# Two-block transformer on one core: the filler products of TensorE are taken out

## The reference, cut to what matters

```python
def reference(x, mem, ...):
    x = first_block(x, mem, ...)
    return second_block(x, c_2, positions_2, ...)

# first_block, one layer
h = _rmsnorm(x, norm_mix); proj = h @ w_in
ya, yb, yc = _mla(...), _fox(...), _chunk_rel(...)      # three kinds of attention
x = x + concat(_rmsnorm(ya), _rmsnorm(yb), _rmsnorm(yc)) @ w_o
x = x + _cross(_rmsnorm(x), _rmsnorm(mem), w_cq, w_ckv, w_co)
h = _rmsnorm(x); gate, up = split(h @ w_gu)
x = x + (silu(gate) * up) @ w_down
# second_block, layers 0 and 1
h = rmsnorm(x) * (1 + sc1) + sh1
y = (gating and pooling) if l == 0 else diff_attention(h, ...)
x = x + g1 * y
h = rmsnorm(x) * (1 + sc2) + sh2
x = x + g2 * peer(h, ...)                # 16384 experts, 8 heads, top 16
return rmsnorm(x)
```

## Time and profile before

| | us |
|---|---|
| median of 3 runs | 2436.04 |
| lowest and highest of them | 2429.02, 2436.44 |
| the profiled execution's own time | 2429.68 |
| its span, first to last instruction | 2427.9 |

### The profile page before, as it was taken

One profiled execution on the slowest core, in us unless ns is written; L12 is line 12 of the kernel. 1 busy time (PEld: TensorE's weight loads), 2 busy tenths in 40 slices (PEclk: granted clock), 3 DMA queues, 4 the chain that ended last, 5 costly groups with the idle time before them and its releaser, 6 DMA issues.

```text
span 2427.9 us, 35824 instructions
## 1 busy us (share of the span) xinstructions
PE 2345.9 (97%) x12736; PEld 1975.7 (81%) x12736; DVE 1799.5 (74%) x3774; ACT 1013.8 (42%) x1568; POOL 297.8 (12%) x228
## 2 busy tenths in 40 slices
PE   8998999999999999999999998999999999999998
PEld 7766998669897888888888777698977888888886
DVE  5446787759998777777777766399987777777776
ACT  4433342232343444444444446222334444444443
POOL 0000000026680000000000000266800000000000
PEclk9999999999999999999999999999999999999999
DMA  7414788863215565655656551232155555655653
GB/s 265 158 70 165 288 324 329 342 252 122 87 45 173 175 190 190 191 190 190 190 191 190 204 191 36 104 115 96 44 166 170 190 190 191 190 190 191 190 191 122
DMA packets 97731, 430.07 MB, mean 177 GB/s; under 512 B 11232, under 2 KB 11872, under 8 KB 90720
## 3 DMA queue, kind: packets, MB, share of 16 engines
q1 hardware_dynamic: 97632, 428.75, 51.7%
HBM read 427.66 MB, written 1.05 MB: 177 GB/s over the span
## 4 chain that ended last, share of the span: by engine, by line
PE 83%; DVE 13%; ACT 2%; DMA 1%; issue 1%; SPq 0%; DVEq 0%; ACTq 0%; PEldq 0%
PE ps L507 43%; PE ps L819 15%; PE ps L822 8%; PE ps L552 5%; PE ps L775 4%; DVE HN L1816 4%; DVE HN L1814 3%; PE ps L565 2%; PE ps L602 1%; PE ps L623 1%; DVE arena L1826 1%; DVE ring_rounded L1834 1%; PE ps L737 1%; DMA ring<-in_stream 1%; PE ps L801 1%
## 5 line engine op out<-in xcount | busy, mean ns | idle before, releaser
L507 PE MATMUL ps<-ring_rounded 128*128 128x512 f32 x3072 | 744.0, 392 | 8.6 <-DVE ring_rounded L1834 8.2
L1834 DVE TENSOR_TENSOR ring_rounded<-ring,ring_rounded 128x1024 fp32r<-128x1024 f32 (+1 forms) x688 | 648.6, 959 | 131.1 <-ACT ring_rounded L1234 104.6
L507 PEld LDWEIGHTS ps<-ring_rounded 128*128 128x128 f32 x3072 | 561.4, 189 | 128.1 <-issue 15.0
L819 PE MATMUL ps<-HNHT_rounded,ring_rounded 128*128 128x512 f32 x1632 | 403.3, 389 | 0.0
L819 PEld LDWEIGHTS ps<-HNHT_rounded,ring_rounded 128*128 128x128 f32 x1632 | 306.2, 188 | 63.4
L1240 ACT ACTIVATE ring_rounded<-ring 128x1024 fp32r<-128x1024 f32 x202 | 214.4, 1061 | 231.4 <-PE ps L507 231.4
L507 PE MATMUL ps<-parts 128*128 128x256 f32 (+2 forms) x1184 | 249.2, 301 | 2.3 <-DVE parts L1400 1.5
L822 PEld LDWEIGHTS ps<-HNHT_rounded,ring_rounded 128*128 128x128 f32 x1632 | 222.6, 190 | 15.9
L822 PE MATMUL ps<-HNHT_rounded,ring_rounded 128*128 128x256 f32 x1632 | 227.6, 282 | 0.0
L1231 ACT ACTIVATE ring<-ps 128x256 f32<-128x256 f32 x204 | 78.3, 384 | 341.6 <-PE ps L822 341.6
L1924 DVE TENSOR_TENSOR ring<-ps,ring 128x256 f32<-128x256 f32 x204 | 86.6, 424 | 168.7 <-ACT ring L1231 168.7
(11 more groups left out here) (258 smaller groups left out, 2836.7 us busy)
## 6 DMA issues: line engine op xcount, KB each, us to landing
ring<-in_experts_u SPq DMA_DIRECT2D x256, 512.0 KB, 3.5
ring<-in_experts_v SPq DMA_DIRECT2D x256, 512.0 KB, 3.4
ring<-in_stream SPq DMA_DIRECT2D x45, 2048.0 KB, 8.9
arena<-in_ada SPq DMA_DIRECT2D x96, 512.0 KB, 7.1
arena<-in_keys SPq DMA_DIRECT2D x2, 1024.0 KB, 13.8
ring<-in_stream SPq DMA_DIRECT2D x1, 1792.0 KB, 7.6
ring<-in_stream SPq DMA_DIRECT2D x1, 1664.0 KB, 8.5
ring<-in_stream SPq DMA_DIRECT2D x1, 1040.0 KB, 19.5
```

Of the source, the lines that this page charges most:

```text
L507: mm = pe.matmul(out_, p, q, start=(first and i == 0), stop=(last and i == 2))
L819: pe.matmul(r3(t, 2), exp_uh[:, j % 2, c], ht_both[:, :, k, :], start=(k == 0), stop=False)
L1834: return dve.tensor_tensor(dst, src, h.bitcast(F32), ALU.subtract)
```

## The change

The table of fillers is emptied. `fill` and its calls stay, and issue nothing. No wait, no buffer and no order of other instructions is altered.

```diff
-FILLERS = {("y", 0): 11, ("cross", 1): 8, ("ffn", 1): 8, ("mix_0", 0): 18, ("peer_0", 1): 10, ("sub", 0): 18, ("peer_1", 1): 10,
-           "mix_1": 20, ("gu", 0): 6, ("probs", 0): 6, ("probs", 6): 6, ("probs", 8): 9, ("values", 15): 5}
+FILLERS = {}
```

## The result

Without the fillers the kernel takes 2441.95 us in the median of 8 runs (2437.57 to 2444.99), against 2431.88 us in the median of 8 runs before (2428.58 to 2436.44). The ratio is 1.0040, with a 95% interval of 1.0028 to 1.0051: slower by 10 us, or 0.4%. The profiled execution took 2440.0 us over a span of 2438.2 us, 10.3 us longer than the one before.

A forecast was written before the change was run, and what follows sets the result against it. TensorE, with 83% of the chain that ended last, was taken to bound the kernel. 15 steps at 1.0 us less 1.1 gave +13.9 us, taken as +12 against the median of 2436.04: 2448 us, range 2440 to 2457 us.

The forecast's parts named there:

- The products themselves: Filler products on TensorE: 130 at twelve places worth 0 us, 5 ahead of unit 15's values a gain of 1.1 us.
- all nine places above 3 us: Filler places whose empty stretch exceeds the longest idle time without a fall; five without a fall now get one each.
- the three doubtful ones: ("probs", 0), ("probs", 6) and ("gu", 0), 6 products each, empty for some 2.6 to 3.0 us; two were counted as falls.
- 15 added steps: Steps of some 3.3 us at clock 0.50 added behind filler places, 15 together.
- 7 + 4 + 4: Added steps: 7 new falls, a second step for 4 of them, one step more at each of four existing falls.
- 1.0 us a step: Price of one added step of low clock on TensorE, taken between 0.8 and 1.5 us, nearer the lower end.
- the lower end I had set: Lowest price of a step, 0.8 us: 8 transposes at "y" take 1.91 us in place of 1.09.
- a sign of being wrong: Second and third waits behind a filler place shrink by what the slow transposes took.
- The sum and the median: Whole kernel: 15 - 1.1 = +13.9 us on the profiled 2429.68 us; +12 against the median 2436.04, 2448 us.
- fewer or cheaper falls: Rival, 15%: no falls at doubtful places, few of two steps; 8 steps at 0.8 less 1.1: +5, 2441 us.
- Fillers don't hold the clock: Rival, 6%: idle time after the last filler decides the clock; only unit 15's 1.1 us goes: 2435 us.
- Transposes leave the clock low: Rival, 5%: transposes don't count as activity; eight steps more at the norms' turns, 1.0 us each: 2456 us.

The follow-up runs named there:

- the longer fillers: Kernel before with more fillers at each place and at some further waits, none ahead of the values of unit 15: 2421.07 us, ratio 0.9956.
- the doubled transposes: Kernel before with 270 filler transposes in place of its 135 filler products, at the same places: ratio 0.9996.
- The halves: Two runs against the kernel before: fillers kept only at the six places ahead of "mix_0", ratio 1.0011; kept only from "mix_0" on, ratio 1.0020.
- the runs with transposes: Kernel before with its 135 filler products replaced by transposes of the constant: 135 transposes, ratio 1.0024; 270 transposes, ratio 0.9996.

## Why the prediction was right, and where it was off

*The products themselves cost nothing at twelve places, 1.1 us at the thirteenth.* Right. Blocks are ready when they were ("cross": 178.12 and 178.11 us), and the run without the unit-15 fillers shows the 1.1 us gone and not taken back.

*Falls at all nine places above 3 us, and at two of the three doubtful ones.* Right in number, if the joined stretch counts as two: "cross", "peer_0", ("probs", 8) and "sub" have new ones, and so do ("probs", 6) and, joined in one stretch of 10.2 us, "ffn" and ("gu", 0); ("probs", 0) has none. What I had not counted is that falls elsewhere come and go: two of before (632.0 and 1502.5 us) are missing, one at 1475.1 is new. Nor is a fall tied to its place: the one at "sub" came with the fillers in place, too, in three profiles.

*15 added steps.* The time at 0.50 grew by 93 - 39 = 54 us, 16 steps of 3.4 us. The forecast was 75 to 85 us in the low stretches; they are 85. The make-up differs from the forecast's 7 + 4 + 4: by the stretches, 12 steps lie in new falls at filler places and 5 more in the four that existed, one is added at the spread, and two are missing. That chance took two away and added one helped the total to come out.

*1.0 us a step.* This is the term that was mis-sized. The loss of 10.3 us and the 1.1 us gained beside it make 11.4 us, over 16 steps 0.7 us each; that is just under the lower end I had set, 0.8. Without the three falls that came and went away from the missing fillers (two gains of 1.7 and 1.5 us, a loss of 1.7), 17 steps at filler places cost 12.9 us, 0.76 us each. The lower end was itself the doubling of 8 transposes, and the table of places shows that where a wait for the second block, or for the copies to HT, follows, even that is hidden. The prediction had named this as a sign of being wrong, that later waits shrink by what the slow transposes took; in part it came, as the wait of 0.79 us at "cross" is gone and the one for the second block at "mix_0" is 0.37 us where it was 1.31. One added step at "y" costs nothing, one at "mix_1" 0.34 us. Steps that run into dense products cost more ("peer_0": 2.6 us for two). The other way, the step price is higher: the longer fillers took away about 20 us at 0.50 and 8.6 us of span. Of this 1.1 us is unit 15, and some 1.6 us more would have gone but for the fillers that are too many at the gates, so it is 7.5 / 20 x 3.4 = 1.3 us a step as measured and 1.5 us without that cost; the one fall at the gates was 1.7 us. These falls were the ones in dense work, 93% busy. A price taken from the rows that exist would have been right for removing falls, and was too high for adding them.

*The sum and the median.* With 0.7 in place of 1.0, 16 x 0.7 - 1.1 = +10 us; that it closes shows nothing, as the 0.7 was worked out from this difference. The 2448 us named are 6 us too high, of which 4 us come from the base: the median of the first three runs was 2436.04 us, of eight 2431.88. The profiled execution was nearer the middle than I took it to be. The change itself, +10 us where +12 was named, came nearer than the time; but a step count close by partly opposite chances and a price too high by a third make some of that luck. The measured 2441.95 us is also 2 us above the lower end, and next to the 2441 us of the rival with fewer or cheaper falls.

*Fillers don't hold the clock* fell with the longer fillers. *Fewer or cheaper falls* was wrong in "fewer" and right in "cheaper" (0.7 us a step, its own price being 0.8); its +5 us is refuted, and its time was hit only because the base was 4 us lower. *Transposes leave the clock low* fell with the doubled transposes (ratio 0.9996, where the lack of all fillers gives 1.0040). The Trainium skill ("TensorE: Matmul & The Clock Gate", Part 4) has transposes not counted as activity; here the measurement decides against it.

What stays open: what a single place is worth in time, "sub" above all. The halves add up only within their intervals of about 0.1%, and which of the borderline waits has a fall differs between profiled executions.

## What to carry to other kernels

Work that fills a wait is free while it ends before the wait does, and what it buys is the clock of the work behind the wait; look at the granted clock in a narrow stretch behind each long wait, since a mean of 0.99 hides it. A filler that stops too early can buy almost nothing (0.34 us at "mix_1", where 4.6 us of fillers left 3.4 us of the wait open), so fill nearly to the end but not past it (0.8 us lost at each of the gates), and check that it stands ahead of the wait, not behind a wait for its own tile. Price a low stretch by what is dense behind it: from nothing, where another wait follows, to 1.7 us per 3.4 us at half clock, in dense work. Before a fall is put down to an edit, look whether the same fall comes and goes in other executions.

## What the runs showed of the hardware

The same wait can have a fall behind it in one execution and none in the next. At the spread of g1_1 TensorE is idle for 2.96 us with the clock staying up in the kernel before, and for 2.97 us with a fall in the changed one; the falls at the gates (632 us) and at unit 15 (1502 us) come and go in the same way. Nor does it take a long wait: with the longer fillers a fall stands at 209 us behind two waits of 0.94 and 1.01 us around the transposes of the cross output; the kernel before has the same two waits and no fall there.

The times go with these falls. Of 29 timed runs of the kernel before, the eight with a mean clock of 0.993 took 2427.7 us on average (2426.66 to 2428.62), the eight with 0.988 or 0.989 2435.9 us (2432.84 to 2437.30). That is 8.2 us for some 22 us more at 0.50, or 1.3 us per 3.4 us. With the longer fillers the clock is 0.996 or 0.997 in all six runs, and they lie within 2.0 us (2420.46 to 2422.45), where the first eight runs of before spread over 7.9 us. What decides whether a fall comes in one execution and not in the next was not tested.

An f32 transpose on TensorE is one instruction of 0.11 us where an f32 product of the same shape is two (1.37 and 2.67 us for eleven, and the runs with transposes).
